# Query projections moved from before the attention into its heads, output splits moved to the last two heads

## The reference

```python
q = _rms((xm @ w_q).reshape(B, T, A_HEADS, 2, A_DH), q_g) * (A_DH ** -0.5)
...
s = jnp.einsum('bqhcd,bkhcd->bhcqk', qblk, k_all).astype(jnp.float32)
p = jax.nn.softmax(jnp.where(mask, s + bias, NEG_BIG), axis=-1)
a = p[:, :, 0] - lam * p[:, :, 1]
return jnp.einsum('bhqk,bkhe->bqhe', a, v_all)
...
o = _rms(o, head_g) * (1 - lam_init)
return (o.reshape(B, T, D_MODEL) @ w_o).astype(xm.dtype)
```

## Time and profile before

| | us |
|---|---|
| median of 3 runs | 1577.12 (1574.72 to 1579.28) |
| profiled execution, device time | 1580.67 |
| its span | 1578.9 |
| PE busy | 1517.3 (96%) |
| DVE busy | 702.4 (44%) |
| POOL busy | 742.2 (47%) |
| ACT busy | 353.0 (22%) |

### The profile page before, as it was taken

How to read it: one execution, slowest core, us unless ns; L and a number is a source line. 1 busy time by engine, 2 the same in 40 slices (tenths; PEclk the granted TensorE clock), 3 DMA queues, 4 the chain that set the end, 5 groups by cost and what they waited for, 6 DMA issues and landing times.

```text
span 1578.9 us, 31838 instructions
## 1 busy us (share of the span) xinstructions
PE 1517.3 (96%) x12614; PEld 1435.4 (91%) x12614; DVE 702.4 (44%) x1312; ACT 353.0 (22%) x789; POOL 742.2 (47%) x424
## 2 busy tenths in 40 slices
PE   5999999999999999999999997888999999999999
PEld 4998898999999999999997895657999999999998
DVE  6503555554342143445572177884554441244421
ACT  4303354221110011113210134775221110011100
POOL 2445332455554554555444440433555555455553
PEclk8999999999999999999999997999999999999999
DMA  9455323433437235353222252220222222222231
GB/s 362 137 167 178 115 74 102 161 134 129 177 139 254 70 126 192 120 190 110 67 69 77 68 214 75 63 83 1 80 80 80 80 100 74 69 89 83 90 114 56
DMA packets 53918, 183.37 MB, mean 116 GB/s; under 512 B 6232, under 2 KB 8672, under 8 KB 53584
## 3 DMA queue, kind: packets, MB, share of 16 engines
q1 hardware_dynamic: 51136, 174.63, 32.4%
q10 hardware_dynamic: 2704, 7.64, 1.3%
HBM read 171.69 MB, written 10.55 MB: 115 GB/s over the span
## 4 chain that ended last, share of the span: by engine, by line
PE 92%; DVE 3%; ACT 2%; issue 1%; POOL 1%; DMA 0%; ACTq 0%; SPq 0%; DVEq 0%; POOLq 0%
PE psum L565 73%; PE psum L611 7%; PE psum L576 3%; PE psum L836 1%; PE psum L928 1%; PE psum L970 1%; PE psum L943 1%; PE psum L915 1%; PE psum L856 1%; ACT sc L1249 1%; PE psum L714 1%; DVE sc L1746 1%; PE psum L743 1%; PE psum L742 0%; PE psum L861 0%
## 5 line engine op out<-in xcount | busy, mean ns | idle before, releaser
L496 POOL TENSOR_SCALAR w_hi<-raw 128x1024 fp32r<-128x1024 f32 (+1 forms) x184 | 210.8, 1146 | 699.5 <-PE psum L565 594.8
L498 POOL TENSOR_TENSOR w_lo<-raw,w_hi 128x1024 fp32r<-128x1024 f32 (+1 forms) x184 | 482.1, 2620 | 15.4
L565 PE MATMUL psum<-act_hi,w_hi 128*128 128x288 f32 x2144 | 470.1, 300 | 4.4 <-POOL w_lo L498 3.0
L565 PE MATMUL psum<-act_hi,w_lo 128*128 128x288 f32 x2144 | 463.5, 298 | 0.0
L565 PE MATMUL psum<-act_lo,w_hi 128*128 128x288 f32 x2144 | 463.1, 297 | 0.0
L565 PEld LDWEIGHTS psum<-act_hi,w_hi 128*128 128x128 f32 x2144 | 348.2, 190 | 10.8 <-issue 7.3
L565 PEld LDWEIGHTS psum<-act_hi,w_lo 128*128 128x128 f32 x2144 | 348.4, 190 | 0.0
L565 PEld LDWEIGHTS psum<-act_lo,w_hi 128*128 128x128 f32 x2144 | 347.6, 190 | 0.0
L565 PE MATMUL psum<-hid_hi,w_hi 128*128 128x288 f32 x704 | 151.1, 296 | 0.0
L565 PE MATMUL psum<-hid_lo,w_hi 128*128 128x288 f32 x704 | 150.8, 296 | 0.0
L565 PE MATMUL psum<-hid_hi,w_lo 128*128 128x288 f32 x704 | 150.7, 296 | 0.0
(11 more groups left out here) (261 smaller groups left out, 1505.6 us busy)
## 6 DMA issues: line engine op xcount, KB each, us to landing
raw<-in_w_stream SPq DMA_DIRECT2D x153, 512.0 KB, 3.5
ada_quad<-in_ada_w SPq DMA_DIRECT2D x48, 512.0 KB, 5.9
raw<-in_w_down SPq DMA_DIRECT2D x32, 704.0 KB, 4.1
ada_ring<-in_ada_w SPq DMA_DIRECT2D x32, 512.0 KB, 4.6
ada_first<-in_ada_w SPq DMA_DIRECT2D x8, 1024.0 KB, 16.0
line_rep<-line SPq DMA_DIRECT2D x8, 352.0 KB, 4.6
line<-line_rep SPq DMA_DIRECT2D x8, 352.0 KB, 5.1
x<-in_x SPq DMA_DIRECT2D x4, 576.0 KB, 5.7
```

Of the source, the lines that this page charges most:

```text
L496: pool.tensor_scalar(hi, src, 1.0, 0.0, ALU.mult, ALU.add).then_inc(hi_split, 1)
L498: pool.tensor_tensor(lo, src, hi.bitcast(F32), ALU.subtract).then_inc(lo_split, 1)
L565: last = mm(psum[:, b + half, 0:n_cols], weights[wp][:, k, :], parts[ap][:, k, half * HT:half * HT + n_cols], start=(k == 0 and n == 0), s ...
```

## The change

Before the attention only the queries of heads 0 and 1 are projected. The query of head p+2 is projected during the five steps of head p, in five parts of 8, 8, 8, 12 and 12 matmuls (`query_part`), one half of the tokens after the other, in PSUM bank 7. DVE evacuates the first half after the third part (`query_first`), which the fourth waits for (`q_half_read`), and the second half after the fifth (`query_second`). The norm of that query is made a head later: squares by ACT in step 0, sums by PE in step 1 (`query_sums`, `query_sums_sample`, banks 6 and 4), copy and guess by ACT (`query_z`, `query_guess`, now by logarithm and exponential), refinement by DVE in steps 2 and 3 (`query_newton`, `query_finish`). Two queries are kept instead of eight. POOL splits one unit's weights in each pass of its loop over heads, and SP loads one in each.

The output of head h, refined, is written where the keys of head h were (`kt_sb`), once these are stored. Outputs 0 to 4 are split in the five steps of head 6, output 5 in head 7, and 6 and 7 after it. The high and low parts go to the activation buffer that held the layer's input (`BUF`), and the attention's own tiles move to the other one. The sample output leaves bank 7 for bank 4, its copy is separate from the prompt's, and the sums of an output come ahead of the turn in step 3. The first two output units advance together, a slice of both at a time, from the step after the last scores (`out_step`). Head 0's tiles are loaded while keys are projected.

```diff
-BUF = [0, 1, 0, 1, 0, 1, 0]
+BUF = [0, 1, 0, 1, 0, 0, 1]
...
+        sc = at("sc", [P, 3, 1024], o1 + 6144)
+        atr = at("atr", [P, 2, 512], o1 + 18432)
+        selr = at("selr", [P, 2, DK], o1 + 22528)
+        q_sb = at("q_sb", [P, 2, T], o1 + 23040)
+        zq, yq, tq = (at(f"q_norm{n}", [P, T], o1 + 23040 + (8 + 4 * n) * T) for n in range(3))
...
+            for u in range(U_AK, U_AQ + 3):
                 load_unit(u)
-                if u == U_AO:
+                if u == U_AK + 2:
                     load_head(0)
             for h in range(1, H):
+                load_unit(U_AQ + 2 + h)
                 load_head(h)
+            load_unit(U_AO + 2)
+            load_unit(U_AO + 3)
...
+            for u0, pairs in ((55, 4), (63, 11), (85, 4), (93, 9)):
                 split_pairs(u0, pairs)
 
             for h in range(-1, H):
                 if h + 1 < H:
+                    split_unit(U_AQ + 3 + h)
...
+            def query_part(n, i0, i1):
+
+                u = U_AQ + n
+                if i0 == 0:
+                    pe.wait_ge(lo_split, u + 1)
+                    if n == 2:
+                        pe.wait_ge(kz_ready, H + 1)
+                    else:
+                        wait_evac(pe, u + 1)
+                elif i0 == 24:
+                    pe.wait_ge(q_half_read, n - 1)
+                for i in range(i0, i1):
+                    half, j = divmod(i, 3 * KT)
+                    wp, ap = SPLIT3[j % 3]
+                    n_cols = HT + 2 * half
+                    last = mm(psum[:, 7, 0:n_cols], w_parts[u % 2][wp][:, j // 3, :],
+                              act[0][ap][:, j // 3, half * HT:half * HT + n_cols], start=(j == 0), stop=(j == 3 * KT - 1))
+                if i1 == 24:
+                    last.then_inc(q_half_mm, 1)
+                elif i1 == 48:
+                    last.then_inc(unit_done, 1)
+
+            def query_sums(n):
+
+                pe.wait_ge(ksq_ready, H + n + 1)
+                pe.wait_ge(kz_ready, H + n)
+                if n >= 3:
+                    pe.wait_ge(oz_ready, n - 2)
+                mm(psum[:, 6, :], cst[:, C_BLK:C_BLK + P], ksq[:, 0:TP], start=True, stop=True)
+
+            def query_sums_sample(n):
+
+                if n >= 2:
+                    pe.wait_ge(at_ready, 5 * n - 6)
+                mm(psum[:, 4, 384:448], cst[:, C_BLK:C_BLK + P], ksq[:, TP:T], start=True, stop=True).then_inc(kms_ready, 1)
...
+            def out_step(k):
+
+                pe.wait_ge(lo_ready[A_O], k + 1)
+                for j in range(2):
+                    s = (U_AO + j) % 2
+                    for n, (wp, ap) in enumerate(SPLIT3):
+                        for half in range(2):
+                            last = mm(psum[:, 2 * s + half, 0:HT], w_parts[s][wp][:, k, :],
+                                      act[BUF[A_O]][ap][:, k, half * HT:(half + 1) * HT],
+                                      start=(k == 0 and n == 0), stop=(k == KT - 1 and n == 2))
+                    if k == KT - 1:
+                        last.then_inc(unit_done, 1)
...
             for g in range(5 * H + 3):
-                if 2 <= g < 5 * H:
+                p, s = divmod(g, 5)
+                if g == 0:
+                    query_part(2, 0, 8)
+                if g < 5 * H:
                     att_scores(g)
+                if p + 2 < H and g > 0:
+                    query_part(p + 2, *((0, 8), (8, 16), (16, 24), (24, 36), (36, 48))[s])
+                if s == 1 and p + 1 < H:
+                    query_sums(p + 1)
+                elif s == 2 and p >= 1:
+                    att_values(g - 3)
+                elif s == 3 and p >= 1:
+                    att_sums(p - 1)
+                if s == 1 and p + 1 < H:
+                    query_sums_sample(p + 1)
+                elif s == 3 and p >= 1:
+                    att_sums_sample(p - 1)
                 if 0 <= g - 2 < 5 * H:
                     att_turn(g - 2)
-                if g >= 3:
+                if g >= 3 and (s != 2 or p == 0):
                     att_values(g - 3)
-                if g >= 8 and (g - 8) % 5 == 0 and g < 5 * H + 3:
-                    att_sums((g - 8) // 5)
-
-            pe.wait_ge(scored, 5 * H)
-            for j in range(2):
-                pe.wait_ge(lo_split, U_AO + j + 1)
-                wait_evac(pe, U_AO + j)
-            for k0, k1 in ((0, KT - 1), (KT - 1, KT)):
-                for j in range(2):
-                    s = (U_AO + j) % 2
-                    for k in range(k0, k1):
-                        pe.wait_ge(lo_ready[A_O], k + 1)
-                        if j == 0 and k == 2:
-                            att_sums(H - 1)
-                        for n, (wp, ap) in enumerate(SPLIT3):
-                            for half in range(2):
-                                last = mm(psum[:, 2 * s + half, 0:HT], w_parts[s][wp][:, k, :],
-                                          act[1][ap][:, k, half * HT:(half + 1) * HT],
-                                          start=(k == 0 and n == 0), stop=(k == KT - 1 and n == 2))
-                    if k1 == KT:
-                        last.then_inc(unit_done, 1)
+                if g >= 5 * H:
+                    if s == 0:
+                        pe.wait_ge(scored, 5 * H)
+                        for j in range(2):
+                            pe.wait_ge(lo_split, U_AO + j + 1)
+                            wait_evac(pe, U_AO + j)
+                    out_step(s)
+            for k in range(3, KT):
+                if k == 5:
+                    att_sums(H - 1)
+                    att_sums_sample(H - 1)
+                out_step(k)
...
+            def query_z(n):
+                sa.wait_ge(kms_ready, H + n + 1)
+                sa.wait_ge(k_ready, H + n)
+                af(zq[:, TP:T], psum[:, 4, 384:448], ACT.Identity, bias=EPSC)
+                af(zq[:, 0:TP], psum[:, 6, :], ACT.Identity, bias=EPSC).then_inc(kz_ready, 1)
+
+            def query_guess(n):
+                sa.wait_ge(kz_ready, H + n + 1)
+                steps(af(yq[:, :], zq[:, :], ACT.Ln))
+                steps.wait()
+                af(yq[:, :], yq[:, :], ACT.Exp, scale=-0.5).then_inc(ky_ready, 1)
...
             for g in range(5 * H):
+                p, s = divmod(g, 5)
+                queries, out = p + 1 < H, p >= 1
                 if g >= 2:
                     att_by_key(g - 2)
+                if s == 1 and queries:
+                    query_z(p + 1)
+                elif s == 2 and out:
+                    out_sample(p - 1)
+                elif s == 3 and out:
+                    z_sample(p - 1)
                 att_exp(g)
-                if g >= 7 and (g - 7) % 5 == 0:
-                    head_out((g - 7) // 5)
-                if g >= 9 and (g - 9) % 5 == 0:
-                    head_guess((g - 9) // 5)
-                if g >= 12 and (g - 12) % 5 == 0:
-                    head_hi((g - 12) // 5)
+                if s == 0 and queries:
+                    kq_square(H + p + 1, U_AQ + p + 1)
+                elif s == 1 and queries:
+                    query_guess(p + 1)
+                elif s == 2 and out:
+                    out_prompt(p - 1)
+                elif s == 3 and out:
+                    z_prompt(p - 1)
+                elif s == 4 and out:
+                    head_guess(p - 1)
+                if p == H - 2:
+                    head_hi(s)
+                elif p == H - 1 and s == 3:
+                    head_hi(5)
             att_by_key(5 * H - 2)
             att_by_key(5 * H - 1)
+            out_sample(H - 1)
+            out_prompt(H - 1)
             head_hi(H - 2)
-            head_out(H - 1)
+            z_sample(H - 1)
+            z_prompt(H - 1)
             head_guess(H - 1)
             head_hi(H - 1)
...
+            def query_first(n):
+
+                ve.wait_ge(q_half_mm, n - 1)
+                tt_(kf[:, n % 2, 0:HT], psum[:, 7, 0:HT], rstd[:, 0:HT], ALU.mult).then_inc(q_half_read, 1)
+
+            def query_second(n):
+                u = U_AQ + n
+                ve.wait_ge(unit_done, u + 1)
+                ve.tensor_copy(shift_sb[:, n % 2, :], psum[:, 7, HT:HT + 2])
+                tt_(kf[:, n % 2, HT:T], psum[:, 7, 0:HT], rstd[:, HT:T], ALU.mult).then_inc(evac[u % 2], 1)
+
+            def query_newton(n):
+                ve.wait_ge(kz_ready, H + n + 1)
+                ve.wait_ge(ky_ready, H + n + 1)
+                steps(tt_(tq[:, :], yq[:, :], yq[:, :], ALU.mult))
+                steps.wait()
+                steps(stt(out=tq[:, :], in0=tq[:, :], scalar=-0.5, in1=zq[:, :], op0=ALU.mult, op1=ALU.mult))
+
+            def query_finish(n):
+                steps.wait()
+                steps(stt(out=yq[:, :], in0=tq[:, :], scalar=1.5, in1=yq[:, :], op0=ALU.add, op1=ALU.mult))
+                steps.wait()
+                stt(out=q_sb[:, n % 2, :], in0=kf[:, n % 2, :], scalar=qgs, in1=yq[:, :],
+                    op0=ALU.mult, op1=ALU.mult).then_inc(k_ready, 1)
...
```

(17 more changed lines are left out.)

139 lines of the change are left out of this document (65 added, 74 removed).

## The result

The changed kernel takes **1584.11 us** (median, 1582.83 to 1585.51) beside 1578.06 for the kernel before on the same chip: ratio 1.0040, 95% interval 1.0026 to 1.0055. I had forecast 1568.6, with a range of 1556 to 1580. The sign was wrong and the time is outside the range.

The account below looks back on a forecast made before the run. Took PE, DVE and ACT, waiting on each other in a ring, to bound attention. Start -13.6, head 6 +7.1, head 7 +1.0, tail -3.0: -8.5 from 1580.67 is 1572.2; that execution being 3.55 above median, 1568.6 (1556 to 1580).

Parts of the forecast that it names:

- Steady heads: Heads 1 to 5: 22.0 us each instead of 22.5, with nearly all of PE's waits staying, at other places.
- rival A: PE fills its waits, so a head costs its PE load, 20.3 us; whole 1560 us; chance 0.17.
- the walk: Following ACT round one steady head: 14.8 us own work, waits for PE 2.7, 0.7, 1.75 and 1.3, total 21.2.
- The start and head 1: From PE's start on head 2's query: 18.2 us to head 1's first score; -13.6 us up to head 6.
- POOL has 6.2 + 3.5 us in a head of 22: Under buffers and loads: POOL's work in a head with projection fits its 22 us; no time charged.
- rival C: DVE, late in the third step behind POOL's split, lengthens heads: 1588 us, or 1579 to 1584 if half; chance 0.15.
- Head 6: No projection, but query 7's norm and five output splits: 22.2 us instead of 15.08, +7.1.
- clock 1.00 from t0 on: Full PE clock expected from PE's start on the query of head 2 (907.1 us in the profile before).
- take the places of the projection parts: In head 6, output splits in steps 1 and 3 replace the projection parts of the heads before.
- rival B: Handovers into busy PE or half clock in head 0: 1 us more in six heads, 2 for clock; 1577; chance 0.22.
- Head 7: The last head keeps the new order of its third step, partly hidden: +1.0 us.
- The tail: Both output units advance a slice at a time, five slices (8 us) ahead of the last head's sums: -3.0 us.

Follow-up runs that it names:

- The one filler that came after the loss: Twelve matmuls of no use in each of six steps of head 0 and the start of head 1, on the kernel before: 1582.0 us (1.0026).
- the fastest version: Changed kernel, DVE's low parts later, POOL's splits for queries 3, 4 held back, last values and sums earlier, useless matmuls in heads 6, 7: 1563.5 us.

## Why the prediction was wrong, step by step

- **Steady heads, right in time, half right in mechanism.** 21.4 to 21.6 us in heads 2 to 5, forecast 22.0; clock 1.00. But not "nearly all of PE's waits stay": PE is busy 20.5 of 21.4 us, its idle time is 0.9 us where it was 2.5, and the head lies between the forecast and rival A's 20.3. In head 2 the chain of waits goes through ACT from 974.2 to 977.2, up to the squares and the query sums, as the walk had it, and then through PE alone up to 992.8. PE waits 0.4 to 0.5 us before the query sums, where I had said 1 to 2.
- **The start and head 1: head 0 right, head 1 missed (4 us).** Start and head 0 took 18.7 us, forecast 18.2. But I went from head 0 to the steady heads, and head 1 is neither: it took 26.0. The step that failed is "POOL has 6.2 + 3.5 us in a head of 22" as the whole account of POOL. The split moved to a place where DVE must evacuate a bank for PE. In steady heads POOL's norm of the last output stands ahead of the split and holds it back; in head 1 there is no such norm yet. Here rival C's mechanism worked, not in the third step of each head but in one head, for 3.4 us (25.97 to 22.62 without it). The rule of the Trainium skill (SBUF — State Buffer, section Who interferes with whom), which I had weighed at 0.7 us a head for the steady ones, showed here at nearly the split's length (2.39 us): 1.95 us on one instruction (2.70 for 0.75), and in the trace with the held split again 1.96 (2.78 for 0.82).
- **Head 6 (+10.4 for +7.1).** With the clock held it takes 23.4, and with the low parts late besides 20.6, where I had 22.2: the sum was near, but it had no term for DVE waiting on ACT's high part. What failed most is "clock 1.00 from t0 on". I let the splits "take the places of the projection parts", which is true of ACT but not of PE: there nothing took their place, PE idled 2.68 us, and the head ran at 0.67 (0.85 in the luckiest trace without a filler, 0.58 in the worst). The earlier trace rows had shown the same at head 0 of before (0.50). A term for it was in rival B, for head 0 alone, where the change in fact cures it. Price: 4.9 us (25.50 to 20.61, both with low parts late).
- **Head 7, the largest miss of one head (+7.3 for +1.0).** It is 15.5 to 15.9 in three traces with a higher clock in its third step, two of them with the low parts where the change has them. So of the 19.8 some 2.5 are the clock, and up to 1.5 lie only at the other side of the line to head 6. The 3.0 to 3.4 that are left over 12.5 are the term that I sized at 1.0. I costed one moved pair of sums and nothing for the splits, which cost 2.1 us (16.12 to 14.06).
- **The tail (+1.8 for -3.0).** I let five slices go ahead of the sums "mostly in that wait". PE is in order: the last sample values stand behind two slices, the sums behind three more, and at half clock the first slice takes 2.9 us. The sums, which started 14.6 us after the last sample scores before (1090.99), start 20.6 us after them (1101.99). With values and sums earlier the tail is 27.0, at full clock 23.7. On the kernel before the interleaving alone brings nothing in the whole.
- **The rest (-4.6 for 0).** "The swap of activation buffers costs nothing" put at nothing a term of 4.6 us, a gain. By this the change without it would be some 10 us slower than before, not 6 (that was not run).

In sum: against the forecast, +2.5 up to head 6, +3.3, +6.3 and +4.8 in the three stages behind, -4.6 in the rest, -1.7 at t0, makes 10.6, the distance between the forecast and measured profile (1570.4 and 1581.0). The largest common cause is the clock, which I had at 1.00 in every stage behind t0 and which was 0.67, 0.74 and 0.90 in the last three. Rival C gave a time near the measured one (1579 to 1584), but by DVE being late in each steady head, which did not happen; that the numbers meet is chance.

## What to carry to other kernels

When work that kept TensorE busy is moved out of a stage or ends a stage early, ask stage by stage what TensorE then does between its short pieces; if nothing, price the stage at half clock, and try to hold the clock with work of no use from the first gap on. The one filler that came after the loss didn't pay here. A trace of such a stage is one execution: before you put a gain of some us down to an edit, look whether the stage has the same clock in both traces. Where a GpSimd instruction is moved, look which DVE instruction it meets and which engine waits behind that one; in head 1 a wait that starts it some 2.5 us later was worth 3.4 us, while the move of a query won 0.9 to 1.1 us in a steady head. Where one engine makes a high part and another the low part, let a step lie between them, and put nothing that the ring needs behind the hand-over.

## What the runs showed of the hardware

- Where the two activation buffers lie changes the time of TensorE matmuls that read neither: 292 or 296 ns in the mean of 1056 matmuls of down units, 4.2 us of a span. It is so in all 15 traces: 292 where the input buffer of the second FFN lies in the upper place, 296 where it lies in the lower; those of the first FFN are at 296 to 297 in all. Exchanging two addresses makes the kernel before 7.4 us faster (1570.7 for 1578.1) with no other edit; in its trace the rest is 6.2 us shorter, and the first scores come 2.6 us earlier. Open why.
- Small DVE instructions are caught as well as large ones. In the fastest version, DVE's negation of two maxima (128 x 2, 0.17 us alone) stands 2.07 us beside the low half of a weight split:

```profile
1043.64 2.07 DVE L1868 TENSOR_SCALAR tiny<-tiny 128x2 f32<-128x2 f32 x1
```
```profile
1043.33 2.35 POOL L505 TENSOR_TENSOR w_lo<-raw,w_hi 128x1024 fp32r<-128x1024 f32 x1
```
- More work can take less time: 60 more matmuls in heads 6 and 7 and 6.1 us less for the whole.
- The same order on PE with the same 2.68 us of idle time can meet either clock: in head 6 the two 512-column matmuls behind it took 2.08 us at half clock in the change and 1.13 at full clock with the low parts late, and the head 22.34 or 25.50 us in two kernels whose order there is the same.
